# Two weight splits moved ahead of the 16x16 inverses, and each inverse built from two 8x8 ones, in a two-layer hybrid transformer block

## The chip, the cores and the metric

The kernel runs on one core of one Trainium2 chip. The metric is the device time of one execution in microseconds. The core has TensorE (matrix products, "PE" in the profile; its weight loads are "PEld"), VectorE ("DVE"), ScalarE ("ACT"), GpSimd ("POOL") and SyncE ("SP", which only issues transfers). They run side by side and wait for each other by semaphores.

## The reference

Two layers work on 256 latent and 256 context tokens of width 1024. In each layer stand a SwiGLU feed-forward, a mixer of three branches (pooling, a gated delta rule in both directions, attention) whose outputs are weighed by sigmoid gates, and a second feed-forward. The change touches the delta rule and what runs beside it. In the delta rule a unit lower-triangular 64x64 system is solved for each of 4 heads, 8 chunks of 64 tokens and 2 directions:

```
A = jnp.where(tril_strict, beta[..., :, None] * kk * decay_mat, 0.0)
lhs = A + jnp.eye(C, dtype=F32)
rhs = jnp.concatenate([v * beta[..., None], k * (beta * jnp.exp(G))[..., None]], axis=-1)
sol = lax.linalg.triangular_solve(lhs, rhs, left_side=True, lower=True, unit_diagonal=True)
```

Beside it stand the projections of the gates, three of width 1024 out of the columns of `w_in`:

```
ga, gb, gc = jnp.split(jax.nn.sigmoid(gates), N_BRANCH, axis=-1)
m = ga * (y_pool @ wa) + gb * (y_dn @ wb) + gc * (y_att @ wc)
```

## The kernel before

All weights come in blocks of 128x1024 numbers through a ring of four slots. For each block a transfer fills `raw`; ScalarE rounds it into `w_hi` (L802); VectorE makes the remainder `w_lo` (the helper `lower`, L1416); and TensorE multiplies with both halves: the three products of L1978, L1979 and L1980 for each of 8 pieces of a block. One such triple is called a *unit* here; it has 512 columns in layer 0 and 256 in layer 1. A block therefore gives TensorE 8 units, and TensorE waits for its `w_lo` before the first.

The order of the instructions on each engine is written out by hand. The 24 gate blocks of a layer (192 units) are filler: a table (`gate_plan`) says how many units TensorE does at each of a row of "gate points", spread over the mixer. Each engine has its own function `gates(p)`. On TensorE it does the units of point p. On ScalarE it takes the sum of each block that is finished at p out of PSUM (L1028) and rounds the block three further on. On VectorE it makes the lower parts for the blocks that were finished at point p - 1: for gate g finished there, the lower part of block g + 3.

The delta rule runs twice in a layer, for two pairs of heads (w = 0 and 1). So there are four such passes, which the text calls S1 (layer 0, w = 0), S2 (layer 0, w = 1), S3 (layer 1, w = 0) and S4 (layer 1, w = 1). Each has three parts:

- Preparation. ScalarE makes decay matrices (L1149), VectorE the matrices `amT` = A (L1738 to L1748), and TensorE does points 0 to 3 in between. Point 4 follows at once on TensorE, with 13 to 19 units. The text calls them points 0 to 4; the change moves what VectorE does at points 3 and 4.
- The small inverses (`sub_blocks`, L1660 to L1698). The 16x16 blocks on the diagonal of all sixteen 128x128 matrices are packed by VectorE (L1728, partitions 0 to 63) and ScalarE (L1158, partitions 64 to 127), turned so that one partition holds one whole 16x16 block (L1668), and inverted there on VectorE alone by 14 elimination steps of two small instructions each (L1684, L1686). They are turned back (L1690) and spread into `tm` by VectorE (L1696) and ScalarE (L1189).
- The solve. TensorE, which has waited for `low` and `lowa` (the two halves of `tm`), doubles the inverse to 32, 64 in three levels (L2344, L2347, L2355), each with replies of ScalarE (L1198) and VectorE (L1788, L1794). The scan over the chunks follows.

The two semaphore waits that matter for TensorE's place are these, behind its points 3 and 4:

```
gates(delta_point(l, w, 3))
gates(delta_point(l, w, PREP_POINTS))
pe.wait_ge(eax.sem, eax.at(l, 4 * w + 4))
pe.wait_ge(low.sem, low.at(l, w + 1))
pe.wait_ge(lowa.sem, lowa.at(l, w + 1))
```

The table gives these lower parts to VectorE at the two points: at point 3 one in S1 and S4 and none in S2 and S3; at point 4 one in each pass. Before, point 3 stands behind the third of the 14 elimination steps, and point 4 behind the last instruction of `sub_blocks`.

## Time and profile before

| | |
|---|---|
| time, median of 3 runs | 2339.87 us (2334.74 to 2342.08) |
| the profiled execution's own time | 2333.58 us |
| its span in the profile | 2331.9 us |
| TensorE busy | 2208.4 us, 95% of the span |
| VectorE busy | 1374.2 us, 59% |
| ScalarE busy | 882.9 us, 38% |
| mean granted TensorE clock | 0.977 of full speed |
| the four passes, from packed blocks to the start of the solve | near 718, 807, 1924 and 2001 us |

Busy time is time in which an instruction is in execution. An engine's idle time is put down to what released it. TensorE is busy nearly always, so the time of the kernel is the sum of TensorE's work and its waits; waits of the other engines cost nothing unless TensorE waits behind them.

### The profile page before, as it was taken

The numbers are of one execution on the slowest core, as the hardware profiler recorded it, in microseconds if no ns is written. First come the engines' busy times: TensorE is split into PE (matmuls) and PEld (weight loads), VectorE is DVE, ScalarE is ACT, GpSimd is POOL, SyncE is SP. The second block draws the span as 40 slices with busy tenths as digits, with TensorE's granted clock in tenths as the row PEclk, the third lists the DMA queues.
The fourth block names the chain that finished last, engine by engine and source line by source line (L and its number), as shares of the span: only waits on it lengthen the run. The fifth ranks groups of instructions, "written<-read, shape, count | busy, mean of one in ns | idle before, by whom it ended". The sixth has DMA issues, their size and how long they took to land.

```text
span 2331.9 us, 33743 instructions
## 1 busy us (share of the span) xinstructions
PE 2208.4 (95%) x12606; PEld 1851.0 (79%) x12606; DVE 1374.2 (59%) x2353; ACT 882.9 (38%) x1376; POOL 236.3 (10%) x300
## 2 busy tenths in 40 slices
PE   4999999999998989999999999999999997798998
PEld 1888878987567767888888898888889776788998
DVE  5777876634446447478875256555356555665554
ACT  2433322433443325343222243332245552355643
POOL 3000022000000200300001100000110001102001
PEclk8999999999999989999999999999999998899999
DMA  6455554322102205245554334444333311144554
GB/s 258 162 184 195 193 175 130 126 85 93 37 32 68 70 27 199 100 165 196 197 188 128 94 123 148 142 143 138 99 126 119 106 55 48 58 161 149 184 172 145
DMA packets 96448, 303.86 MB, mean 130 GB/s; under 512 B 10592, under 2 KB 17248, under 8 KB 95328
## 3 DMA queue, kind: packets, MB, share of 16 engines
q1 hardware_dynamic: 76912, 230.87, 30.1%
q0 software_dynamic: 18720, 69.21, 8.7%
q10 hardware_dynamic: 720, 2.44, 0.3%
q8 instruction: 67, 1.10, 0.2%
q14 instruction: 29, 0.24, 0.0%
HBM read 291.99 MB, written 10.49 MB: 130 GB/s over the span
## 4 chain that ended last, share of the span: by engine, by line
PE 55%; DVE 4%; ACT 2%; issue 1%; DMA 1%; SPq 0%; ACTq 0%; DVEq 0%
PE ps L1978 16%; PE ps L1980 16%; PE ps L1979 16%; DVE w_lo L1416 1%; PE ps L2229 1%; PE ps L2250 1%; PE ps L2344 1%; PE ps L2355 0%; PE ps L2347 0%; PE ps L2416 0%; PE ps L2414 0%; PE ps L2238 0%; PE ps L2166 0%; DVE gate_in L1871 0%; ACT w_hi L802 0%
## 5 line engine op out<-in xcount | busy, mean ns | idle before, releaser
L1978 PE MATMUL ps<-h_hi,w_hi 128*128 128x512 f32 (+1 forms) x2176 | 781.8, 359 | 61.7 <-DVE w_lo L1416 43.3
L1979 PE MATMUL ps<-h_lo,w_hi 128*128 128x512 f32 (+1 forms) x2176 | 763.7, 351 | 0.0
L1980 PE MATMUL ps<-h_hi,w_lo 128*128 128x512 f32 (+1 forms) x2176 | 763.7, 351 | 0.0
L1416 DVE TENSOR_TENSOR w_lo<-raw,w_hi 128x1024 fp32r<-128x1024 f32 (+2 forms) x416 | 475.2, 1146 | 464.3 <-ACT w_hi L802 458.8
L802 ACT ACTIVATE w_hi<-raw 128x1024 fp32r<-128x1024 f32 (+2 forms) x416 | 404.6, 974 | 619.3 <-DMA raw<-in_w_down 316.9
L1978 PEld LDWEIGHTS ps<-h_hi,w_hi 128*128 128x128 f32 x2176 | 420.4, 193 | 153.5 <-DVE w_lo L1416 47.5
L1980 PEld LDWEIGHTS ps<-h_hi,w_lo 128*128 128x128 f32 x2176 | 420.8, 193 | 52.2
L1979 PEld LDWEIGHTS ps<-h_lo,w_hi 128*128 128x128 f32 x2176 | 421.1, 194 | 49.4
L1978 PE MATMUL ps<-a_hi,w_hi 128*128 128x512 f32 (+1 forms) x1050 | 362.4, 345 | 9.5 <-DVE buf_b L1873 3.6
L1980 PE MATMUL ps<-a_hi,w_lo 128*128 128x512 f32 (+1 forms) x1050 | 360.7, 343 | 0.0
L1979 PE MATMUL ps<-a_lo,w_hi 128*128 128x512 f32 (+1 forms) x1050 | 359.2, 342 | 0.0
L1448 DVE CUSTOM_DVE_ANT_0 ps<-ada,c_wide 128x1024 f32<-128x1024 f32 x256 | 319.4, 1248 | 7.5 <-DMA ada<-in_w_ada_t 2.4
L1978 PEld LDWEIGHTS ps<-a_hi,w_hi 128*128 128x128 f32 x1050 | 197.2, 188 | 38.6 <-DVE buf_b L1873 5.8
L1979 PEld LDWEIGHTS ps<-a_lo,w_hi 128*128 128x128 f32 x1050 | 197.3, 188 | 26.7
L1980 PEld LDWEIGHTS ps<-a_hi,w_lo 128*128 128x128 f32 x1050 | 197.7, 188 | 25.8
L696 POOL DMA_DIRECT2D ada<-in_w_ada_t x128 | 67.9, 531 | 775.3 <-DVE ada_sum L1448 768.1
L920 ACT ACTIVATE a_hi<-buf_b 128x512 f32 (+3 forms) x88 | 50.9, 579 | 204.8 <-DVE buf_b L1434 204.8
L658 POOL TENSOR_TENSOR buf_a<-x 128x512 f32<-128x512 f32 (+1 forms) x40 | 51.8, 1296 | 247.2 <-DVE x L1422 246.4
L1439 DVE TENSOR_TENSOR a_lo<-buf_b,a_hi 128x512 f32 (+3 forms) x88 | 54.7, 622 | 26.2 <-ACT a_hi L920 26.1
L1422 DVE SCALAR_TENSOR_TENSOR x<-ps,mod,x 128x256 f32<-128x256 f32 (+1 forms) x68 | 30.4, 480 | 60.6 <-PE ps L1980 60.6
L1434 DVE TENSOR_TENSOR buf_b<-buf_a,ps 128x512 f32<-128x512 f32 (+1 forms) x88 | 54.1, 615 | 8.2 <-PE ps L1980 8.2
L704 POOL MEMSET tm<- 128x2048 f32 x4 | 7.2, 1806 | 470.7 <-DVE g_cum L1701 470.7
(253 smaller groups left out, 1844.8 us busy)
## 6 DMA issues: line engine op xcount, KB each, us to landing
raw<-in_w_up SPq DMA_DIRECT2D x176, 512.0 KB, 3.8
ada<-in_w_ada_t POOLq DMA_DIRECT2D x128, 512.0 KB, 3.9
raw<-in_w_down SPq DMA_DIRECT2D x64, 384.0 KB, 3.1
raw<-in_w_gate SPq DMA_DIRECT2D x48, 512.0 KB, 3.3
raw<-in_w_down SPq DMA_DIRECT2D x64, 320.0 KB, 2.9
raw<-in_w_proj SPq DMA_DIRECT2D x32, 512.0 KB, 3.3
raw<-in_w_merge SPq DMA_DIRECT2D x16, 512.0 KB, 3.8
raw<-in_w_out SPq DMA_DIRECT2D x16, 512.0 KB, 3.2
```

Source lines behind the costliest of these rows:

```text
L658: link(pool.tensor_tensor(buf_a[:, 1, 0:n], xk, xk, ALU.mult))
L696: pool.dma_start(ada[:, j, :], a["w_ada_t"][ADA_FIRST - KD + 2 * r + j]).then_inc(s_ada[j], 16)
L802: return act.activation(w_hi[:, j % RING, 0:cols], raw[:, j, 0:cols], ACT.Copy)
L920: act.activation(a_hi[:, q, 0:n], buf_b[:, j, 0:n], ACT.Copy).then_inc(s_ahi, 1)
L1416: vec.tensor_tensor(w_lo[:, j % RING, 0:cols], raw[:, j, 0:cols], w_hi[:, j % RING, 0:cols].bitcast(F32), ALU.subtract).then_inc(s_lo, 1)
L1422: last = vec.scalar_tensor_tensor(x[:, k, cols], ps[:, bank, cols], mod[:, l, (3 * which + 2) * KD + k, i:i + 1], x[:, k, cols], ALU.mult, ...
L1434: vec.tensor_tensor(buf_b[:, j, 0:n], buf_a[:, j, 0:n], ps[:, 2 * j + 1, 0:n], ALU.mult).then_inc(s_mul, 1)
L1439: vec.tensor_tensor(a_lo[:, q, 0:n], buf_b[:, j, 0:n], a_hi[:, q, 0:n].bitcast(F32), ALU.subtract).then_inc(s_alo, 1)
L1448: vec.tensor_tensor_reduce(ps[:, 6:8, :].rearrange("p b n -> p (b n)"), ada[:, j, :], c_wide[:, i, :], 1.0, 0.0, ALU.mult, ALU.add, ada_su ...
L1978: pe.matmul(out, wh, rows_hi[:, i, c], start=first, stop=False)
L1979: pe.matmul(out, wh, rows_lo[:, i, c], start=False, stop=False)
L1980: return pe.matmul(out, wl, rows_hi[:, i, c], start=False, stop=last)
```

## The change

It has three parts, all inside `sub_blocks` and the packing ahead of it.

1. Both calls `gates(...)` on VectorE, points 3 and 4, now stand directly behind the set-up of the small inverses and ahead of all elimination steps.
2. The masks with which the turned blocks were taken apart (four instructions over 256 elements) are applied while packing: the copies become multiplications by a column of 0 or -1 (`minus_rows`), on VectorE and on ScalarE. Behind the transposition one addition of two halves takes the place of two masked instructions; the rest of the set-up stays.
3. Each 16x16 inverse is made from two 8x8 ones. Six elimination steps (in place of 14) work on both 8x8 diagonal blocks at once; then the corner is the product of the two inverses with the block between them: two multiplications over 512 elements, each followed by a sum over groups of eight.

```diff
@@ packed
-            to = sub_pack[r, :].rearrange("p (i z t h) -> p z t h i", z=2, t=8, h=2)[:, :, 4 * h:4 * h + 4]
-            old = amT[r, 4 * h:4 * h + 4, r].rearrange("p t (h i) -> p t h i", h=2)
-            return [(to[:, z], old) for z in range(2)]
+            out = []
+            for e in range(2):
+                c = q * QUAD + e * SUB
+                to = sub_pack[r, :].rearrange("p (i z t e) -> p e z t i", z=2, t=8, e=2)[:, e, :, 4 * h:4 * h + 4, :]
+                old = amT[r, 4 * h:4 * h + 4, c:c + SUB].rearrange("p (o t) n -> p o t n", o=1)
+                out.append((to, old.to_broadcast([QUAD, 2, 4, SUB]), minus_rows(e, r)))
+            return out
+        def sub_halves(r0, rows, c0, cols, row_step=SUB, col_step=1):
+            return bass.AP(xm, 2 * P + r0 * SUB + c0, [[8 * P, P], [(SUB + 1) * SUB // 2, 2], [row_step, rows], [col_step, cols]])
+        def sub_terms(at, left):
+            if left:
+                return bass.AP(xm, at, [[8 * P, P], [SUB, SUB // 2], [0, SUB // 2], [1, SUB // 2]])
+            return bass.AP(xm, at, [[8 * P, P], [0, SUB // 2], [1, SUB // 2], [SUB, SUB // 2]])
@@ ScalarE, pack
-                            last = act.activation(to, old, ACT.Copy)
+                            last = act.activation(to, old, ACT.Copy, scale=minus)
@@ VectorE, sub_blocks
-                    link(vec.tensor_scalar(t, raws[:, :, 0, :], half_minus(0, 1), None, ALU.mult))
-                    link(vec.scalar_tensor_tensor(t, raws[:, :, 1, :], half_minus(1, 1), t, ALU.mult, ALU.add))
-                    link(vec.scalar_tensor_tensor(t, raws_t[:, :, 0, :], half_minus(0, 0), t, ALU.mult, ALU.add))
-                    link(vec.scalar_tensor_tensor(t, raws_t[:, :, 1, :], half_minus(1, 0), t, ALU.mult, ALU.add))
+                    link(vec.tensor_tensor(sums, raws[:, :, 0, :], raws[:, :, 1, :], ALU.add))
+                    link(vec.tensor_scalar(sub_t, sub_sum, side_rows(1), None, ALU.mult))
+                    link(vec.scalar_tensor_tensor(t, sub_sum.rearrange("p (i j) -> p j i", i=SUB), side_rows(0), t,
+                                                  ALU.mult, ALU.add))
                     link(vec.tensor_tensor(sub_t, sub_t, low_mask, ALU.mult))
                     link(vec.tensor_copy(sub_t[:, 0:SUB * SUB:SUB + 1], ones[:, 0:SUB]))
-                    for j in range(1, SUB - 1):
-                        if j == SUB // 4:
-                            gates(delta_point(l, w, PREP_POINTS - 1))
-                        size = [P, SUB - 1 - j, j]
-                        part = sub_part[:, 0:size[1] * j].rearrange("p (i c) -> p i c", c=j)
-                        link(vec.tensor_tensor(part, t[:, j + 1:SUB, j:j + 1].to_broadcast(size),
-                                               t[:, j:j + 1, 0:j].to_broadcast(size), ALU.mult))
-                        link(vec.tensor_tensor(t[:, j + 1:SUB, 0:j], t[:, j + 1:SUB, 0:j], part, ALU.add))
+                    gates(delta_point(l, w, PREP_POINTS - 1))
+                    gates(delta_point(l, w, PREP_POINTS))
+                    half = SUB // 2
+                    for j in range(1, half - 1):
+                        rows = half - 1 - j
+                        part = sub_part[:, 0:2 * rows * j].rearrange("p (b i c) -> p b i c", b=2, c=j)
+                        link(vec.tensor_tensor(part, sub_halves(j + 1, rows, j, j, col_step=0),
+                                               sub_halves(j, rows, 0, j, row_step=0), ALU.mult))
+                        link(vec.tensor_tensor(sub_halves(j + 1, rows, 0, j), sub_halves(j + 1, rows, 0, j), part, ALU.add))
+                    corner, last = 2 * P + half * SUB, 2 * P + half * SUB + half
+                    terms = sub_part.rearrange("p (i x k) -> p i x k", i=half, x=half)
+                    made = sub_sum[:, 0:half * SUB].rearrange("p (i x) -> p i x", x=SUB)[:, :, 0:half]
+                    link(vec.tensor_tensor(terms, sub_terms(corner, True), sub_terms(2 * P, False), ALU.mult))
+                    link(vec.tensor_reduce(made, terms, AXX, ALU.add))
+                    link(vec.tensor_tensor(terms, sub_terms(last, True), sub_terms(0, False), ALU.mult))
+                    link(vec.tensor_reduce(t[:, half:SUB, 0:half], terms, AXX, ALU.add))
...
                     last.then_inc(low.sem, 1)
-                    gates(delta_point(l, w, PREP_POINTS))
@@ VectorE, pack
-                            last = vec.tensor_copy(to, old)
+                            last = vec.tensor_scalar(to, old, minus, None, ALU.mult)
```

VectorE in S1, from the set-up of the inverses to the first lower part. `xm` is the memory in which `sub_pack`, `sub_raw`, `sub_sum`, `sub_t` and `sub_part` lie, and `w_lo` rows are the lower parts. Before:

```order
L1674 SCALAR_TENSOR_TENSOR xm<-xm,masks 128x256
L1675 SCALAR_TENSOR_TENSOR xm<-xm,masks 128x256
L1676 SCALAR_TENSOR_TENSOR xm<-xm,masks 128x256
L1677 TENSOR_TENSOR xm<-xm,masks 128x256
L1678 COPY xm<-ones 128x16
L1684 TENSOR_TENSOR xm<-xm 128x14
L1686 TENSOR_TENSOR xm<-xm 128x14
L1684 TENSOR_TENSOR xm<-xm 128x26
L1686 TENSOR_TENSOR xm<-xm 128x13x2
L1684 TENSOR_TENSOR xm<-xm 128x36
L1686 TENSOR_TENSOR xm<-xm 128x12x3
L1416 TENSOR_TENSOR w_lo<-raw,w_hi 128x1024
```

The same place of the change:

```order
L1682 STREAM_TRANSPOSE xm<-xm 128x512
L1686 TENSOR_TENSOR xm<-xm 128x256
L1687 TENSOR_SCALAR xm<-xm,masks 128x256
L1688 SCALAR_TENSOR_TENSOR xm<-xm,masks 128x256
L1690 TENSOR_TENSOR xm<-xm,masks 128x256
L1691 COPY xm<-ones 128x16
L1430 TENSOR_TENSOR w_lo<-raw,w_hi 128x1024 x2
L1698 TENSOR_TENSOR xm<-xm 128x12
L1700 TENSOR_TENSOR xm<-xm 128x2x6
```

The set-up has one instruction less, and two lower parts in a row stand where the first elimination step stood.

VectorE in S1, the end of `sub_blocks` up to the first reply to the solve. Before:

```order
L1684 TENSOR_TENSOR xm<-xm 128x14
L1686 TENSOR_TENSOR xm<-xm 128x14
L1687 TENSOR_SCALAR xm<-xm,masks 128x256
L1688 SCALAR_TENSOR_TENSOR xm<-xm,masks 128x256
L1690 STREAM_TRANSPOSE xm<-xm 128x512
L1692 ISA
L1696 TENSOR_SCALAR tm<-xm,masks 32x16x16 x5
L1416 TENSOR_TENSOR w_lo<-raw,w_hi 128x1024
L1788 TENSOR_TENSOR xm<-ps,masks 128x512 x2
```

And of the change:

```order
L1698 TENSOR_TENSOR xm<-xm 128x12
L1700 TENSOR_TENSOR xm<-xm 128x2x6
L1704 TENSOR_TENSOR xm<-xm 128x512
L1705 TENSOR_REDUCE xm<-xm 128x8x8
L1706 TENSOR_TENSOR xm<-xm 128x512
L1707 TENSOR_REDUCE xm<-xm 128x8x8
L1708 TENSOR_SCALAR xm<-xm,masks 128x256
L1709 SCALAR_TENSOR_TENSOR xm<-xm,masks 128x256
L1711 STREAM_TRANSPOSE xm<-xm 128x512
L1713 ISA
L1717 TENSOR_SCALAR tm<-xm,masks 32x16x16 x5
L1808 TENSOR_TENSOR xm<-ps,masks 128x512 x2
```

The four instructions of the corner are new, the tail is the same, and no lower part stands behind it any more. TensorE's, ScalarE's and GpSimd's rows stand in the order of before; ScalarE's packing reads `masks` as well.

## Rows read from the trace of the kernel before

**Rows 1.** The page, the chain that ended last, shares by engine.

```profile
PE 55%; DVE 4%; ACT 2%; issue 1%; DMA 1%; SPq 0%; ACTq 0%; DVEq 0%
```

**Rows 2.** PE's waits in 690:850 and 1850:2100: us in total, times, longest.

```profile
PE ps L1978 <- DVE w_lo L1416: 14.3, 3, 8.2
...
PE ps L1978 <- DVE w_lo L1416: 23.6, 3, 12.3
```

**Rows 3.** Timeline of PE in S1: start us, us, engine, line, names, shape, count.

```profile
720.83 0.39 PE L1980 MATMUL ps<-h_hi,w_lo 128*128 128x512 f32 x1
...
721.51 0.39 PE L1980 MATMUL ps<-h_hi,w_lo 128*128 128x512 f32 x1
724.73 0.50 PE L1978 MATMUL ps<-h_hi,w_hi 128*128 128x512 f32 x1 [2.83 <-DVE w_lo L1416]
...
735.33 0.50 PE L1978 MATMUL ps<-h_hi,w_hi 128*128 128x512 f32 x1 [3.27 <-DVE w_lo L1416]
...
740.46 1.03 PE L2344 MATMUL ps<-consts,tm 128*128 128x128 f32 x8
...
745.93 1.04 PE L2344 MATMUL ps<-consts,tm 128*128 128x128 f32 x8
```

**Rows 4.** Timeline of DVE in S1.

```profile
718.31 0.70 DVE L1668 STREAM_TRANSPOSE xm<-xm 128x512 f32<-128x512 f32 x1
...
722.11 0.17 DVE L1684 TENSOR_TENSOR xm<-xm 128x14 f32<-128x14 f32 x1
...
723.45 1.23 DVE L1416 TENSOR_TENSOR w_lo<-raw,w_hi 128x1024 fp32r<-128x1024 f32 x1
724.59 0.20 DVE L1684 TENSOR_TENSOR xm<-xm 128x44 f32<-128x44 f32 x1
...
729.86 0.35 DVE L1687 TENSOR_SCALAR xm<-xm,masks 128x256 f32<-128x256 f32 x1
```

**Rows 5.** Timeline of ACT in S1.

```profile
715.42 2.79 ACT L1158 ACTIVATE xm<-amT 32x128 f32<-32x128 f32 x8
...
732.14 2.06 ACT L1189 ACTIVATE tm<-xm,masks 32x256 f32<-32x256 f32 x3 [8.67 <-DVEq L1692]
```

**Rows 6.** Timeline of PE in S2, S3 and S4.

```profile
823.13 0.80 PE L1978 MATMUL ps<-h_hi,w_hi 128*128 128x512 f32 x1 [8.17 <-DVE w_lo L1416]
...
830.34 1.03 PE L2344 MATMUL ps<-consts,tm 128*128 128x128 f32 x8
...
1940.22 0.58 PE L1978 MATMUL ps<-h_hi,w_hi 128*128 128x256 f32 x1 [12.29 <-DVE w_lo L1416]
...
1943.59 1.36 PE L2344 MATMUL ps<-consts,tm 128*128 128x128 f32 x8
...
2007.05 0.58 PE L1978 MATMUL ps<-h_hi,w_hi 128*128 128x256 f32 x1 [6.20 <-DVE w_lo L1416]
...
2017.62 0.58 PE L1978 MATMUL ps<-h_hi,w_hi 128*128 128x256 f32 x1 [5.09 <-DVE w_lo L1416]
2018.43 1.91 PE L2344 MATMUL ps<-consts,tm 128*128 128x128 f32 x8
...
2026.00 1.04 PE L2344 MATMUL ps<-consts,tm 128*128 128x128 f32 x8
```

**Rows 7.** Groups by line and shape: count, busy us, mean ns, idle before.

```profile
L1633 DVE TENSOR_REDUCE stat<-ps 128x1 f32<-128x512 f32 x32 | 22.1, 690 | 20.2 <-PE ps L2229 20.1
L1738 DVE TENSOR_TENSOR amT<-em,beta 128x512 f32<-128x512 f32 x8 | 5.5, 691 | 27.2 <-ACT em L1149 27.2
L1675 DVE SCALAR_TENSOR_TENSOR xm<-xm,masks 128x256 f32<-128x256 f32 x4 | 2.8, 688 | 0.1
L1674 DVE SCALAR_TENSOR_TENSOR xm<-xm,masks 128x256 f32<-128x256 f32 x4 | 1.9, 485 | 0.1
...
L832 ACT ACTIVATE out_t<-buf_a,nfin 128x256 f32<-128x256 f32 x8 | 3.6, 500 | 1.7 <-DVE buf_a L1316 1.5
L859 ACT ACTIVATE buf_b<-x 128x256 f32<-128x256 f32 x8 | 3.3, 417 | 31.3 <-DVE x L1335 31.3
```

More of the change, by code:

```diff
@@ L192, in side_rows, with minus_rows @@
             return masks[:, C_HALF - N_KEEP + 2 + z:C_HALF - N_KEEP + 3 + z]
-        def half_minus(h, z):
-            return masks[:, C_HALF - N_KEEP + 4 + 2 * h + z:C_HALF - N_KEEP + 5 + 2 * h + z]
+        def minus_rows(h, r):
+            return masks[r, C_HALF - N_KEEP + 4 + h:C_HALF - N_KEEP + 5 + h]
         def half_rows(h, r):
@@ L1156, in pack @@
                     for q in range(PACKED, len(quads)):
-                        for to, old in packed(h, q):
-                            last = act.activation(to, old, ACT.Copy)
+                        for to, old, minus in packed(h, q):
+                            last = act.activation(to, old, ACT.Copy, scale=minus)
                     last.then_inc(cmp.sem, 1)
@@ L1669, in sub_blocks @@
                     raws = sub_raw.rearrange("p (i h j) -> p i h j", i=SUB, h=2)
-                    raws_t = sub_raw.rearrange("p (i h j) -> p j h i", i=SUB, h=2)
                     sums = sub_sum.rearrange("p (i j) -> p i j", i=SUB)
                     t = sub_t.rearrange("p (i j) -> p i j", i=SUB)
-                    link(vec.tensor_scalar(t, raws[:, :, 0, :], half_minus(0, 1), None, ALU.mult))
-                    link(vec.scalar_tensor_tensor(t, raws[:, :, 1, :], half_minus(1, 1), t, ALU.mult, ALU.add))
@@ L1726, in pack @@
                     for q in range(PACKED):
-                        for to, old in packed(h, q):
-                            last = vec.tensor_copy(to, old)
+                        for to, old, minus in packed(h, q):
+                            last = vec.tensor_scalar(to, old, minus, None, ALU.mult)
                     link(last)
@@ L2512, in constants @@
         c[:, C_HALF + 2 + h] = i // SUB % 2 == h
-        for z in range(2):
-            c[:, C_HALF + 4 + 2 * h + z] = -1.0 * ((i % 2 == h) & (i // SUB % 2 == z))
+        c[:, C_HALF + 4 + h] = -1.0 * (i // SUB % 2 == h)
     s = np.arange(SUB)
```

## The prediction

> **What bounds the kernel now.** I read the chain that ended last first: TensorE holds most of it [rows 1]. So a change pays where TensorE waits, and only there. The table of who waited for whom, taken over both mixers, names one large cause: six waits for a lower part `w_lo`, 14.3 + 23.6 = 37.9 us [rows 2]. The timelines then show where they lie: all six stand inside or right behind the small inverses of the four passes S1 to S4 [rows 3, 6].
>
> S1 shows the pattern. TensorE runs units at 0.68 us each (720.83 to 721.51), stops at 721.90 for the lower part of point 3, restarts at 724.73 when VectorE's L1416 of 723.45 ends, does 8 units, stops again at 732.06 for the lower part of point 4 and restarts at 735.33 [rows 3, 4]. It does the last 5 units and begins the solve at 740.46 without any wait. The inverses themselves are ready before that: ScalarE's half of `tm` ends at 732.14 + 2.06 = 734.20 [rows 5]. So now the gate block is late and the inverse is not. If the block comes earlier, the inverse is late next. That exchange is what has to be worked out.
>
> A second cost sits on top of each wait. The 8 units behind 724.73 take 7.33 us, where 8 x 0.68 = 5.44 would do, and the 5 units behind 735.33 take 5.13 for 3.40 [rows 3]. So a restart after some 3 us of idleness costs TensorE a further 1.7 to 1.9 us, and one after 8.17 us costs 7.21 - 7 x 0.68 = 2.4 us [rows 6]. The solve suffers too: in S4, 0.8 us behind a restart, its first level takes 2026.00 - 2018.43 = 7.57 us, and in S1, with TensorE undisturbed, 745.93 - 740.46 = 5.47 us [rows 3, 6].
>
> **The change, part by part.** I count from T, the start of VectorE's transposition (718.31 in S1).
>
> *Packing.* The same number of instructions over the same elements, now with a scale. On VectorE I set this at nothing. On ScalarE a copy of 256 elements with a scale column takes 0.500 us and a plain activation 0.417 [rows 7], so +0.083 us each. In S1 eight copies run into T back to back (2.79 us from 715.42, ending 0.1 us before T) [rows 5]: T comes 0.6 us later. Elsewhere four copies count: 0.3 us. The other bound is nothing at all, since the scaled copies of L1189, twice as long, take 2.06 / 3 = 0.69 us, no more than two of L1158 at 0.35 [rows 5].
>
> *Set-up.* It took 722.11 - 718.31 = 3.80 us [rows 4]. One of the two instructions that read across rows goes (0.688) [rows 7]; the others keep their size or shrink slightly: 3.1 us.
>
> *Lower parts.* An L1416 occupies VectorE 724.59 - 723.45 = 1.14 us, and TensorE restarts 1.28 us after its start [rows 3, 4]. S1 and S4 now have two in front of the inverses, S2 and S3 one. Their inputs: ScalarE's order is unchanged, and in S1 its packing ends at 718.2, so the two roundings that stand next in its order come before VectorE gets to their lower parts, at 722.0 and 723.1.
>
> *Elimination.* 28 small instructions took 729.86 - 722.11 - 1.14 = 6.61 us, 0.236 each [rows 4]. Twelve remain, with fewer elements but one more dimension: 12 x 0.236 = 2.8 us.
>
> *Corner.* The trace has no such product. The nearest from below is an ordinary 512-element product, 0.691 us. But its right operand steps by 16 numbers per element. L1675, which reads that way, takes 0.688 for 256 elements, L1674 beside it 0.485: 0.203 us more per 256 [rows 7]. So 0.691 + 2 x 0.203 = 1.10 us, which I take because the pattern is the same; from above, twice L1675, 1.38. A sum over 512 elements takes 0.690 (L1633, to one result) [rows 7]; with 64 results I take the same, and 1.10 from above. Together 2 x 1.10 + 2 x 0.69 = 3.6, with the links between them 3.7 us; between 2.8 and 5.0.
>
> The Trainium skill ("VectorE: DVE Perf Modes", the section on the TRN2 errata) gives (N + 151) / 0.96 ns for such a product whatever its pattern, so 0.69 us. For 256 elements it would give 0.42, and L1675 shows 0.688, so the rows speak against it here. By it the corner would be 0.8 us shorter in each pass and the gain 3.3 us larger. "SBUF — State Buffer", the section "Door 1: The DMA port swizzle", says that reads that leave a 16-byte line at every element pay a penalty, which is the rows' side.
>
> *Tail.* Unchanged: 734.20 - 729.86 = 4.34 us up to ScalarE's half [rows 4, 5], and 0.1 us to TensorE.
>
> Sum from T to the solve's release: 3.1 + 2.8 + 3.7 + 4.3 + 0.1 = 14.0, plus 1.14 for each lower part in front: 16.3 us in S1 and S4, 15.2 in S2 and S3, plus the 0.6 or 0.3 of packing. Before, TensorE's last restart stood 735.33 - 718.31 = 17.02 us behind T in S1. S4 has the same instructions; S2 and S3 have one L1416 less, 15.88. That gives the old T of the other passes from their restarts [rows 6].
>
> - S1: solve at 718.31 + 16.3 + 0.6 = 735.2, before 740.46: 5.3 us earlier. TensorE's units would be done at 732.1 (restart at 718.31 + 0.6 + 3.1 + 1.28 = 723.3, then 13 x 0.68), so it waits 3.1 us for the inverse.
> - S2: 823.13 - 15.88 + 15.5 = 822.8, before 830.34: 7.6 us. TensorE's block is there in time (it was wanted at 823.13 - 8.17 = 814.96, the lower part ends near 812), 7 units end at 819.7, and it waits 3.0 us.
> - S3: 1940.22 - 15.88 + 15.5 = 1939.8, before 1943.59: 3.8 us. TensorE waits some 8 us.
> - S4: 2017.62 - 17.02 + 16.6 = 2017.2, before 2018.43: 1.2 us. The first wait of 6.20 shrinks to about 4.4 (restart at 2000.6 + 0.3 + 3.1 + 1.28), and another of 6 us stands before the solve.
>
> Together 17.9 us. In all four passes the solve now waits for the inverse, so it begins behind an idle TensorE, and the slow restart falls into it: 1.7 us in S1 and in S2 (waits of 3 us). In S3 2.1 us, what S4 shows over S1: a level right behind a restart would lose a little more, and S3's lost a little already (1.36 for 1.03 in its first row), which I take as equal. In S4 0.4 more than now. Together 5.9 us. The dips that the units no longer have are in the starts above already.
>
> Net 17.9 - 5.9 = 12.0 us. Moved transfers: the order of their issue is unchanged and slots become free earlier, so I cost them at nothing; TensorE's wait would show if they were late. Behind the solve all is as before and TensorE is the bound, so the 12.0 us should stay. Profiled execution: 2333.58 - 12.0 = 2321.6 us. It ran 6.3 us below the median, so for a median 2339.87 - 12.0 = **2328 us**.
>
> **Rivals.**
> - *Forecast* (0.70): the inverse becomes the late one in each pass; 8 to 16 us, 2324 to 2332.
> - *The short chain* (0.14): products at the 0.69 us of L1738 (-3.3 us over four passes), steps at 0.21 (-1.2), no price for the scale (-1.5), and 3 us of idleness not slowing a solve whose products stand between replies anyway (-3.4): 21 us, 2318.5. For it: the solve's products are short. Against it: L1675.
> - *Only the gate wait pays* (0.12): products at 1.38, sums at 1.10 (+5.5 us over the passes), and a slow restart after the remaining 1.4 us wait in S1 (+1.9): a gain of 4.6, 2335. Within 0.3% (7 us, about what a measurement can tell).
> - *The corner eats it* (0.04): the corner's four instructions lie behind both lower parts and in front of `low`, and every us there delays all four solves. At 3.0 us above my 3.7 the gain is gone; at 4.8 above, 8.5 in all, the kernel is 7 us slower: 2347. That needs products of some 3.5 us each, five times an ordinary one; nothing in the rows reads that badly.
> - That the gate blocks don't come earlier at all would need ScalarE's rounding over 1 us late; the order forbids it.
>
> The likeliest is 2328; the range 2317 to 2335 takes in the short chain and most of the third case. Faster by over 0.3%: 0.84; within: 0.12; slower: 0.04.
>
> **What would show it.** In the profile after, the waits for `w_lo` in both mixers should fall from 37.9 to about 7 us (1.4 in S1, 1.1 in S3, 4.4 in S4, none in S2), and four waits of TensorE for `tm` should appear in front of the solve, of 3, 3, 8 and 6 us. The transposition should come 0.3 to 0.6 us later behind ScalarE, the products should take 1.1 us, the sums 0.7, and the first level of the solve 7 us or more in place of 5.5. The prediction is wrong if a product takes over 2 us, if the restart costs nothing, or if the freed time turns up as a wait behind the mixer.

## The result and the profile after

| | before | changed kernel |
|---|---|---|
| median of the first comparison, us | 2337.88 (2334.74 to 2342.08, 4 runs) | 2316.32 (2311.71 to 2319.58, 4 runs) |
| ratio | | 0.9913, 95% interval 0.9893 to 0.9933 |
| profiled execution: span / time, us | 2331.9 / 2333.58 | 2315.7 / 2317.6 |
| mean granted clock | 0.977 | 0.981 |

The change makes the kernel faster by 0.9%. Forecast were 2328 us and a range from 2317; it came out 11.7 us below the first and just under the second. With all later comparisons the kernel before has a median of 2333.9 (76 runs) and the changed one 2317.0 (16 runs in three sets): the gain is 17 us, with a 95% interval of 15.7 to 19.0 from resampling the two sets. The first four runs of before were high ones, so the 21.6 us between the first two medians say too much.

The table of waits, PE alone, in the stretches 690:870 and 1850:2100 of the changed kernel, answers [rows 2]:

```profile
PE ps L2364 <- ACT tm L1203: 5.1, 2, 2.6
PE ps L2422 <- DVE vnew L1833: 1.8, 2, 1.5
PE ps L1998 <- DVE w_lo L1430: 1.1, 1, 1.1
...
PE ps L2364 <- ACT tm L1203: 14.9, 2, 8.3
PE ps L1998 <- DVE w_lo L1430: 5.1, 2, 4.4
```

The waits for `w_lo` fell from 37.9 to 6.2 us, and four waits of the solve (L2364) for `tm` took their place, 20.0 us in all: block and inverse have exchanged roles. The wait for `vnew` is not new; in the kernel before it stands at 860.02 us with 1.53 us, just outside the stretch read there. VectorE's timeline in S1 (start us, us, line, names, shape, count) answers [rows 4]:

```profile
717.53 0.71 DVE L1682 STREAM_TRANSPOSE xm<-xm 128x512 f32<-128x512 f32 x1
...
720.51 2.36 DVE L1430 TENSOR_TENSOR w_lo<-raw,w_hi 128x1024 fp32r<-128x1024 f32 x2
722.79 0.17 DVE L1698 TENSOR_TENSOR xm<-xm 128x12 f32<-128x12 f32 x1
...
725.34 1.05 DVE L1704 TENSOR_TENSOR xm<-xm 128x512 f32<-128x512 f32 x1
726.43 0.69 DVE L1705 TENSOR_REDUCE xm<-xm 128x64 f32<-128x512 f32 x1
727.15 1.05 DVE L1706 TENSOR_TENSOR xm<-xm 128x512 f32<-128x512 f32 x1
728.24 0.69 DVE L1707 TENSOR_REDUCE xm<-xm 128x64 f32<-128x512 f32 x1
728.96 0.35 DVE L1708 TENSOR_SCALAR xm<-xm,masks 128x256 f32<-128x256 f32 x1
```

From T at 717.53: set-up 2.98 us, two lower parts 2.28, twelve steps 2.55, corner 3.62. ScalarE in the same place answers [rows 5]:

```profile
714.21 3.30 ACT L1172 ACTIVATE xm<-amT,masks 32x128 f32<-32x128 f32 x8
...
731.24 2.06 ACT L1203 ACTIVATE tm<-xm,masks 32x256 f32<-32x256 f32 x3 [8.97 <-DVEq L1713]
```

Eight scaled copies take 3.30 us where eight plain ones took 2.79. TensorE in S1, S2 and S4 answers [rows 3, 6]; the wait ahead of an instruction stands in brackets:

```profile
721.79 0.50 PE L1998 MATMUL ps<-h_hi,w_hi 128*128 128x512 f32 x1 [1.10 <-DVE w_lo L1430]
...
733.44 1.06 PE L2364 MATMUL ps<-consts,tm 128*128 128x128 f32 x8 [2.48 <-ACT tm L1203]
...
740.59 1.04 PE L2364 MATMUL ps<-consts,tm 128*128 128x128 f32 x8
...
816.97 1.94 PE L2364 MATMUL ps<-consts,tm 128*128 128x128 f32 x8 [2.58 <-ACT tm L1203]
...
1987.29 0.48 PE L1998 MATMUL ps<-h_hi,w_hi 128*128 128x256 f32 x1 [4.41 <-DVE w_lo L1430]
...
1998.87 1.94 PE L2364 MATMUL ps<-consts,tm 128*128 128x128 f32 x8 [6.59 <-ACT tm L1203]
```

The same eight first products of the solve take 1.03 us undisturbed [rows 3] and 1.94 behind the waits of S2 and S4. Windows over the first level of the solve in S1 to S4 (length, then busy us of each engine with counts, then granted clock, DMA share, GB/s) show why:

```profile
733.44:740.59 7.15, 7.15 (x48) 7.07 (x49) 2.07 (x3) 2.73 (x4) 0.00 (x0) 0.76 0.10 37
816.97:823.95 6.98, 6.98 (x48) 6.90 (x49) 2.07 (x3) 2.73 (x4) 0.00 (x0) 0.78 0.10 38
1922.76:1929.81 7.05, 7.05 (x49) 6.97 (x49) 2.07 (x3) 2.51 (x4) 0.00 (x0) 0.77 0.07 21
1998.87:2007.08 8.21, 8.21 (x48) 8.13 (x49) 2.07 (x3) 2.52 (x4) 0.00 (x0) 0.66 0.06 18
```

and of the kernel before, where S1 and S4 stand for the two cases:

```profile
740.46:745.93 5.47, 5.47 (x49) 5.39 (x48) 2.07 (x3) 2.25 (x3) 0.00 (x0) 1.00 0.00 0
...
2018.43:2026.00 7.57, 7.57 (x50) 7.49 (x49) 2.07 (x3) 2.25 (x3) 0.00 (x0) 0.71 0.01 2
```

The "slow restart" of the prediction is the clock: a level that runs wholly at the full level (2.4 GHz, 1.00) takes 5.47 us, and one that spends about half of its time or more at the lower (1.2 GHz) takes 7 or more.

To compare kernels whose passes stand at other places, I measure each pass by itself, from the first product of its third group of decay rows (703.09 us in S1 of the kernel before; TensorE does gate point 0 ahead of it) to the start of the solve and to the second level. From the timelines of the two kernels, in us:

```
                 to the solve: S1    S2    S3    S4     to its second level: S1    S2    S3    S4    sum
before                      37.37 38.28 29.77 29.04                       42.84 43.75 35.57 36.61  158.8
changed                     31.56 30.22 25.53 27.44                       38.72 37.21 32.58 35.65  144.2
```

The solve starts 5.8, 8.1, 4.2 and 1.6 us earlier in its pass (19.7 together), its first level gives back 5.1, and 14.6 remain. TensorE's last product comes 16.2 us earlier (2322.9 and 2306.7). The stretch up to that product in S1 (703.1 and 701.9) was 1.2 us of this, the rest between and behind the passes 0.4, both of unchanged work.

### The profile page after: what moved, and what is told of

Read it like the earlier page. It is cut to its first block, busy times and chain, and to the rows that moved or that the text cites. A ratio compares the mean times of both kernels' runs of the same rounds, so it can differ in the third digit from the quotient of the medians.

```text
span 2315.7 us, 33693 instructions
## 1 busy us (share of the span) xinstructions
PE 2204.7 (95%) x12606; PEld 1848.5 (80%) x12606; DVE 1372.9 (59%) x2301; ACT 884.4 (38%) x1376; POOL 236.1 (10%) x300
## 4 chain that ended last, share of the span: by engine, by line
PE 56%; DVE 4%; ACT 2%; DMA 1%; issue 1%; SPq 0%; ACTq 0%; DVEq 0%
PE ps L1998 17%; PE ps L2000 16%; PE ps L1999 16%; DVE w_lo L1430 1%; PE ps L2249 1%; PE ps L2270 1%; PE ps L2364 1%; PE ps L2367 1%; PE ps L2375 1%; PE ps L2436 0%; PE ps L2434 0%; DMA gate_in<-gate_sums 0%; PE ps L2258 0%; PE ps L2314 0%; PE ps L2186 0%
## 5 line engine op out<-in xcount | busy, mean ns | idle before, releaser
L1998 PE MATMUL ps<-h_hi,w_hi 128*128 128x512 f32 (+1 forms) x2176 | 775.4, 356 | 30.1 <-DVE w_lo L1430 11.7
```

What stands on the lines that cost most here:

```text
L1998: pe.matmul(out, wh, rows_hi[:, i, c], start=first, stop=False)
```

## The experiments

They ran in four sets, each on one chip with its own runs of the kernel before. The table has for each the parts of its profile and its times, in us: the profile up to the start of the first pass, the four passes as above, everything else up to TensorE's last product, and the medians.

```
                                up to S1  passes   else    median (runs)      ratio, 95% interval
kernel before                    703.1    158.8   1461.0
before again                     702.6    160.4   1467.2   2334.36 (12)       1.0002  0.9985-1.0018
change                           701.9    144.2   1460.7   2316.32 (4)        0.9913  0.9893-0.9933
change again                     703.1    144.5   1457.8   2316.30 (6)        0.9923  0.9902-0.9945
change, third                    705.7    143.7   1460.4   2317.62 (6)        0.9931  0.9911-0.9950
lower parts only                 703.3    147.3   1457.0   2321.55 (10)       0.9952  0.9935-0.9969
lower parts only, again          701.4    148.5   1456.6   2317.46 (6)        0.9937  0.9917-0.9958
inverse and packing only         703.4    153.5   1468.6   2336.04 (12)       1.0003  0.9986-1.0019
old packing                      702.1    148.3   1456.3   2318.41 (4)        0.9932  0.9909-0.9956
corner made longer               701.0    157.8   1467.8   2336.11 (10)       1.0005  0.9989-1.0021
corner in another order          704.2    143.5   1461.2   2318.97 (4)        0.9935  0.9912-0.9957
change + fill                    702.6    137.5   1459.9   2311.77 (6)        0.9910  0.9892-0.9929
change + fill, again             705.0    137.6   1460.4   2313.24 (6)        0.9912  0.9895-0.9930
lower parts + fill               701.7    141.2   1460.1   2312.04 (5)        0.9905  0.9889-0.9921
lower parts + fill, again        699.6    141.3   1459.8   2312.55 (6)        0.9914  0.9895-0.9932
change + fill + fill in a scan   704.0    137.6   1459.9   2314.19 (6)        0.9916  0.9900-0.9932
before + fill                    700.6    152.9   1469.8   2329.05 (12)       0.9975  0.9963-0.9987
```

The passes repeat within 1.6 us for one kernel; the other two columns, where all kernels do the same work, vary by 6 and 13. A single profile shows a pass well and the total badly.

### The change again, and before again

No edit. 

> The changed kernel once more, in more rounds. The two profiles at hand give the four delta passes a gain of 14.6 us (each pass from its own packing to the second level of its solve) and the rest of the program 1.6 us, while the medians lie 20 to 22 us apart. Theory A (the passes are all, the rest is the chance of single executions): ratio 0.9935 to 0.9945, so 13 to 15 us, and a second profile whose passes repeat those of the first within 0.5 us each. Theory B (something outside the passes gains 5 us or more in most executions): ratio near 0.9913 again.

> The kernel before itself, for a second profile and for what two equal kernels differ by. Ratio 1.000 within 0.002. Theory A: its passes repeat the first profile's within 0.5 us each, and the rest of the program differs from it by several us, at places where TensorE restarts slowly by chance. Theory B: the rest repeats as well.

The change repeated its gain at ratio 0.9923, between the two theories; its passes came out at 144.5 us in all, with S3's 0.9 us longer, more than the 0.5 expected. The kernel before repeated itself (1.0002). In its second profile the passes differ by 1.6 us, S1's by 1.3 and not the 0.5 expected, and the rest by 6.2. Where the 6.2 comes from is visible in the scan behind S2. Windows over its first 300 products, the same in every kernel, of before and of before again:

```profile
835.85:876.58 40.73, 38.95 (x303) 30.60 (x301) 17.88 (x40) 10.33 (x18) 4.54 (x10) 0.92 0.06 21
```

```profile
836.98:882.82 45.84, 44.05 (x302) 33.05 (x301) 17.88 (x40) 10.33 (x18) 4.55 (x10) 0.79 0.06 18
```

The same work takes 5.1 us more at a mean clock of 0.79 than at 0.92. Windows over the first 600 products of this place, in the change, in before again and in the kernel with the lower parts alone (below):

```profile
823.95:929.50 105.55, 101.86 (x603) 81.16 (x601) 65.46 (x94) 43.65 (x54) 4.54 (x10) 0.97 0.36 123
```

```profile
837.00:949.91 112.91, 109.22 (x602) 85.22 (x601) 65.44 (x94) 43.75 (x54) 4.55 (x10) 0.89 0.34 115
```

```profile
827.28:930.85 103.57, 98.97 (x603) 79.44 (x602) 65.44 (x94) 43.69 (x54) 4.54 (x10) 1.00 0.37 125
```

This is less a matter of chance than it looks. The 600 products took 105.5 us in all three profiles of the change and in all four of the fill with early lower parts, 103.6 in both of the lower parts alone, in the old packing and in the other order of the corner. Only the kernel before, among those profiled more than once, shows two values (105.6 and 112.9). The inverse alone, the long corner and before with fill took 110.0 to 111.4.

### The two halves of the change

The lower parts ahead, with the old packing, set-up and elimination:

```diff
+                    gates(delta_point(l, w, PREP_POINTS - 1))
+                    gates(delta_point(l, w, PREP_POINTS))
                     for j in range(1, SUB - 1):
-                        if j == SUB // 4:
-                            gates(delta_point(l, w, PREP_POINTS - 1))
...
-                    gates(delta_point(l, w, PREP_POINTS))
```

> Part 1 of the change alone: both lower parts stand ahead of the 14 elimination steps, packing and inverse are those of before. From the transposition to the solve: 3.80 set-up + 1.14 for each lower part + 6.61 steps + 4.34 tail + 0.1 = 17.1 us in S1 and S4, 16.0 in S2 and S3. The solve would start 5.0, 7.1, 3.2 and 0.6 us earlier than before, 15.9 us together, less 5 us for slow restarts in the solve: 11 us, three quarters of the passes' 14.6. If instead the shorter inverse were what pays, this would gain under 4 us.

And the new packing and inverse with the lower parts where they were:

```diff
-                    gates(delta_point(l, w, PREP_POINTS - 1))
-                    gates(delta_point(l, w, PREP_POINTS))
                     for j in range(1, half - 1):
+                        if j == SUB // 4:
+                            gates(delta_point(l, w, PREP_POINTS - 1))
...
+                    gates(delta_point(l, w, PREP_POINTS))
```

> Parts 2 and 3 alone: masks in the packing and 8x8 inverses, with the lower parts where they stood before (behind the third elimination step, and behind the end). The last restart of TensorE comes 0.4 (packing) + 3.0 + 1.1 (where there is a part at point 3) + 2.55 + 3.62 + 4.2 + 1.3 behind the old transposition: 16.2 us in S1 and S4 and 15.1 in S2 and S3, where it was 17.02 and 15.88. So about 0.8 us in each pass, 3.2 us in all, within 0.3% or barely over. If the inverse's length is what counts, it would gain over 8 us.

The lower parts alone bring 2321.55 and, in a second set, 2317.46: 2320.3 over 16 runs, 14 of the 17 us. The starts of the solve moved by 5.0, 7.1, 3.2 and 0.7 us, as expected. Its waits in the two stretches are those of the change with a longer wait for `tm`:

```profile
PE ps L2343 <- ACT tm L1189: 6.5, 2, 3.6
...
PE ps L2343 <- ACT tm L1189: 15.1, 2, 8.8
PE ps L1977 <- DVE w_lo L1416: 6.4, 2, 4.9
```

The inverse alone brings nothing (1.0003): the waits for `w_lo` are still 12.4 + 22.4 us, since the last block stands behind an inverse that is only a little shorter. Its passes are 5.3 us shorter in the profile (3.2 were expected), and the rest of that execution is 7.6 us longer, with 45.1 us for the 300 products behind S2. So whether the shorter passes are a gain that chance covers can't be read from one profile; twelve timed runs show none.

### The packing's share

The change with the plain copies and the four masked instructions of before, and the new inverse:

```diff
-                            last = act.activation(to, old, ACT.Copy, scale=minus)
+                            last = act.activation(to, old, ACT.Copy)
-                    link(vec.tensor_tensor(sums, raws[:, :, 0, :], raws[:, :, 1, :], ALU.add))
-                    link(vec.tensor_scalar(sub_t, sub_sum, side_rows(1), None, ALU.mult))
...
+                    link(vec.tensor_scalar(t, raws[:, :, 0, :], half_minus(0, 1), None, ALU.mult))
+                    link(vec.scalar_tensor_tensor(t, raws[:, :, 1, :], half_minus(1, 1), t, ALU.mult, ALU.add))
...
```

> The change without its part 2: copies in the packing and four masked instructions behind the transposition, as before; the 8x8 halves and both lower parts ahead of them stay. ScalarE's packing ends 0.3 to 0.5 us earlier, the set-up takes 3.8 in place of 3.0 us: the solve starts 0.4 us later in each pass, 1.6 us in all, ratio 0.993. If the scaled copies cost what they save, or more, this equals or beats the changed kernel.

The solve starts 0.41, 0.56, 0.50 and 0.49 us later, 2.0 us together: the new packing wins this, the shorter set-up less its own price. The time (0.9932 beside 0.9913, 0.9923 and 0.9931 for the change) can't tell 2 us.

### The corner, made longer and turned round

The last rival named the corner as the one place that could turn the gain into a loss. Two products and a sum done twice make it 2.9 us longer:

```diff
                     link(vec.tensor_reduce(made, terms, AXX, ALU.add))
                     link(vec.tensor_tensor(terms, sub_terms(last, True), sub_terms(0, False), ALU.mult))
+                    link(vec.tensor_tensor(terms, sub_terms(corner, True), sub_terms(2 * P, False), ALU.mult))
+                    link(vec.tensor_reduce(made, terms, AXX, ALU.add))
+                    link(vec.tensor_tensor(terms, sub_terms(last, True), sub_terms(0, False), ALU.mult))
```

> The changed kernel with three of the corner's instructions done twice, with the same operands and results: a product, its sum and the other product, 1.05 + 0.69 + 1.05 + 0.1 for the links = 2.9 us more in each pass. Theory: the inverse is the last thing before the solve in all four passes, so all of it is on the path: 11.6 us more than the changed kernel, ratio near 0.9975. If TensorE's own units still ended last in some pass, that pass would take nothing from it, and the loss would be 8.7 us or less.

The solves start 2.9, 2.9, 2.9 and 2.8 us later, microsecond for microsecond, and the first levels lose another 2. The passes take 13.6 us more, and the time is back at that of before (1.0005). That is 19 us more than the change and not the 11.6 expected: the rest of the profile is 7.1 us longer too, 4.4 of it in the 600 products behind S2. The corner stands on the path in all four passes. The rival's turning point, 3.0 us above the forecast, came true as a number; the corner's own 11.4 us would have left some 6 us of the gain, and the clock took the rest.

The other edit turns the order of the products round, so that it is the sum that reads in steps and not the product:

```diff
-                return bass.AP(xm, at, [[8 * P, P], [SUB, SUB // 2], [0, SUB // 2], [1, SUB // 2]])
+                return bass.AP(xm, at, [[8 * P, P], [SUB, SUB // 2], [1, SUB // 2], [0, SUB // 2]])
...
-                    terms = sub_part.rearrange("p (i x k) -> p i x k", i=half, x=half)
+                    terms = sub_part.rearrange("p (i k x) -> p i k x", i=half, x=half)
+                    terms_x = sub_part.rearrange("p (i k x) -> p i x k", i=half, x=half)
```

> The changed kernel, with the corner's terms laid out so that both products read and write runs of eight neighbours, and the sums step by eight numbers in their place. If it is the read that steps at every element that costs a product 1.05 in place of 0.69 us: products 0.69, and the sums rise from 0.69 to about 1.05, with the total unchanged at 3.6 us. If the sum doesn't mind, the corner takes 2.9 us, 0.7 less per pass and 2.9 us in all.

Groups by line and shape, first of the change, then of this kernel:

```profile
L1704 DVE TENSOR_TENSOR xm<-xm 128x512 f32<-128x512 f32 x4 | 4.2, 1042 | 0.1
L1706 DVE TENSOR_TENSOR xm<-xm 128x512 f32<-128x512 f32 x4 | 4.1, 1034 | 0.1
L1705 DVE TENSOR_REDUCE xm<-xm 128x64 f32<-128x512 f32 x4 | 2.7, 686 | 0.1
```

```profile
L1706 DVE TENSOR_REDUCE xm<-xm 128x64 f32<-128x512 f32 x4 | 4.4, 1105 | 0.1
...
L1705 DVE TENSOR_TENSOR xm<-xm 128x512 f32<-128x512 f32 x4 | 2.8, 692 | 0.1
```

The product falls from 1.04 to 0.69 us and the sum rises from 0.69 to 1.10: the price of the stepped read moves with the read, and the corner stays at 3.6 us.

This kernel shows one thing more. TensorE at the start of the solve in S2, and the window over its first level:

```profile
819.56 1.06 PE L2365 MATMUL ps<-consts,tm 128*128 128x128 f32 x8 [2.73 <-ACT tm L1203]
```

```profile
819.56:825.06 5.50, 5.50 (x48) 5.42 (x49) 2.07 (x3) 2.73 (x4) 0.00 (x0) 1.00 0.13 48
```

Behind a wait of 2.73 us, longer than the 2.58 us of the change in S2, this level ran wholly at the full clock. It is the only one: the other 31 first levels of the eight profiles without fill in which the solve waits for the inverse took 6.9 to 8.4 us. So such a wait nearly always brings the low clock here, and not always.

### Filling TensorE's waits

If the slow first levels come from the idleness ahead of them, TensorE only has to be kept busy. These kernels put products whose result nobody reads into bank 2, free at that point, in front of the waits:

```diff
+                def fill(n):
+                    for _ in range(n):
+                        pe.matmul(ps[:, 2, :], ident_r, h_hi[:, 0, :], start=True, stop=True)
...
+                    fill((10, 11, 35, 35)[2 * l + w])
                     pe.wait_ge(low.sem, low.at(l, w + 1))
```

and 18 more in front of one block of S4.

> The changed kernel, and while TensorE waits for the inverse it multiplies the identity with a tile of the layer's input into a bank that the solve then overwrites (10, 11, 35 and 35 products of 512 columns in S1 to S4), and 18 more in S4 while it waits for the lower part. The products' results are not used. If idleness of TensorE is what brings the slow restarts: the solve's first level falls from 7.0 to 8.2 us to about 5.5 in all four passes, S4's units behind the lower part run at 0.36 each, the low clock near the passes is gone from the profile, and the kernel gains some 7 to 9 us over the changed one (ratio to before near 0.989). If the clock falls for another reason: no gain, or a loss where the added products delay the solve.

TensorE in S1, with the ten products and what is left of the wait:

```profile
731.54 2.49 PE L2185 MATMUL ps<-h_hi,masks_r 128*128 128x512 f32 x10
734.31 0.41 PE L2373 MATMUL ps<-consts,tm 128*128 128x128 f32 x2 [0.28 <-ACT tm L1203]
```

and the windows over the first levels:

```profile
734.31:739.81 5.50, 5.50 (x48) 5.42 (x49) 2.07 (x3) 2.73 (x4) 0.00 (x0) 1.00 0.13 48
...
1995.93:2001.43 5.50, 5.50 (x48) 5.42 (x49) 2.07 (x3) 2.52 (x4) 0.00 (x0) 1.00 0.09 27
```

5.50 us and clock 1.00 in all four passes, with the solves starting within 0.3 us of where they did. The passes become 6.6 us shorter, and over two sets the time is 2312.7 (12 runs) against 2317.0: 4.2 us, interval 2.3 to 5.8, less than the 7 to 9 expected. So the price of the restarts was the clock's, and it can be had back.

The same for the kernel before, which waits elsewhere:

```diff
+                fills = {(0, 14): 11, (0, 15): 13, (0, 21): 34, (1, 14): 52, (1, 20): 25, (1, 21): 29}
...
+                            if (l, g) in fills:
+                                pe.wait_ge(eax.sem, eax.at(l, 4 if g < 20 and (l, g) != (0, 21) else 8))
+                                fill(fills[l, g])
                             pe.wait_ge(s_lo, b + 1)
```

> The kernel before, with 11, 13, 34, 52, 25 and 29 products of 512 columns that nobody reads, put where TensorE waits longest for w_lo of the third and fourth gate point; nothing else is changed. Theory (the low clock of the solves comes from the idleness ahead of them, and its price of 1.7, 2.1, 1.8 and 2.5 us in the four first levels can be had back without any gain on VectorE): first levels 5.5 us in each pass where they read 5.5 to 7.6, the time at the low clock down from 92.7 us by 20 or more, solve starts unmoved within 0.3 us, gate blocks ahead of the solve faster too; about 2325, ratio 0.9965. Rival (in the kernel before the blocks between the waits bring the clock back in time, so filling gives nothing, and each product that runs on past the arrival of w_lo costs): 2333 to 2336, ratio 1.000 to 1.001.

All first levels take 5.47 us and S2's solve starts 2.1 us earlier, S3's 1.3. S1 gave nothing (42.96 for 42.84). The expectation set a price of 1.7 and 2.1 us on the first levels of S1 and S2, which already took 5.47; what S2 gave lies ahead of its solve. Over the whole execution the time at the low clock fell from 108 us (the expectation had 92.7) to 90. The passes are 5.9 us shorter, the ratio is 0.9975 (0.9963 to 0.9987), 5.8 us. Filling alone is worth a third of what the change gives, and it does not replace it: with the fill in both, the kernel before has 2329.05 and the changed one 2312.7, still 16 us apart.

Six more fill products in S2's scan, where TensorE waits 1.5 us for `vnew`, on top of the fill of the change:

```diff
                             gates(delta_point(l, w, PREP_POINTS + 2 * t))
+                            if l == 0 and w == 1 and t == 1:
+                                fill(6)
                             pe.wait_ge(vn.sem, vn.at(l, 3 * w + t))
```

> The change with the fill of before, and 6 more such products in the second pass's scan, where TensorE waits 1.5 us for the new values of the second tile and a stretch of 7 to 24 us at the low clock follows in each profile so far. Theory (that short idleness starts the long low stretches behind the second pass): granted clock 1.00 from there to the end of the scan, 3 to 4 us less in the profile, 2309 against 2311.8, ratio 0.9895. Rival (the low stretch has another start, and the 6 products add at most their own end): the low stretch is still there, 2311.8 to 2312.5.

Windows over the 300 products behind S2, of the change with fill and of this kernel:

```profile
821.77:862.47 40.70, 38.91 (x302) 30.50 (x302) 17.87 (x40) 10.33 (x18) 4.55 (x10) 0.92 0.07 20
```

```profile
823.17:861.94 38.77, 37.49 (x308) 29.96 (x308) 17.88 (x40) 10.34 (x18) 4.55 (x10) 1.00 0.07 21
...
861.94:905.00 43.06, 41.16 (x202) 33.01 (x203) 28.20 (x35) 22.65 (x25) 0.00 (x0) 0.96 0.57 196
```

The low stretch is gone from there (1.9 us), but the clock fell later in the same scan (0.96), and the time is not better: 2314.19. The lower parts alone (38.76 us at 1.00, twice), the old packing and the corner in another order have the same wait of 1.5 us there and no low clock behind it, so the wait by itself does not bring it. In the other kernels without these six products the clock falls within 3 us behind the wait. Whether it takes part is neither shown nor excluded; as a means of gaining time the fill here failed.

### What the new inverse is worth

With the fill the price of the clock is out of the way, so the two halves can be compared again. The edit is the fill (14, 14, 38, 38 and 20 products) in the kernel with the lower parts alone.

> Lower parts early with the inverse and packing of before, and such products (14, 14, 38, 38 ahead of the solve, 20 in front of one block of the last pass). Beside the same fill with the whole change (2311.8) it shows what the new inverse is worth where the clock is no matter. Theory: what it is worth is the start of the solve, 0.8 to 1.0 us in each pass, 3.7 in all: 2315.5, ratio 0.9925; first levels 5.5 us. Rival (the 5.2 us between the lower parts alone and the whole change was mostly the shorter idle stretch ahead of the solve, which the fill gives anyway): 2312, ratio 0.991.

> The whole change with the fill, again. Both theories: 2311.8, ratio 0.991.

> The lower parts alone with the fill, again. Theory P (the inverse pays what it starts the solve earlier, 3.7 us, whatever the clock does): 3.7 us above the whole change with the fill, ratio 0.9925. Rival C (it pays mostly by the shorter idle stretch ahead of the solve): within 1.5 us of the whole change with the fill, ratio 0.991.

> The change, a third time. Both theories: 4.5 us above the fill, 2316.3, ratio 0.992.

> The lower parts alone, again. Theory P: 3.7 us and the difference of the restarts (first levels 5.5 to 7.4 in both), so 4 above the change, 2320, ratio 0.994. Rival C: 5 to 6 above it, 2321.5 to 2322, ratio 0.995.

In the profile the theory holds each time: the solves start 0.8, 1.0, 1.0 and 0.9 us later with the old inverse, first levels are at 1.00, the passes 3.7 us longer. In the times it fails: 2312.0 for the lower parts (11 runs) and 2312.7 for the change (12 runs), a difference of -0.7 us with an interval of -1.9 to 1.7, where 3.7 were expected. Without the fill the two sets disagree (5.2 us and -0.2); pooled it is 3.4, interval 0.9 to 6.8. The rival, that the inverse pays by the shorter idle stretch, would explain the filled times and the first set without fill, but not the second set (-0.2) and not the profiles, where the first levels without the fill are nearly alike in both kernels (29.4 us in the change, 28.8 and 30.0 with the lower parts alone).

The unchanged stretch up to S1 took 702.6, 705.0 and 704.0 us in the three filled profiles with the new inverse and 701.7 and 699.6 in the two with the old. Windows over 430:442 in it, change with fill and lower parts with fill:

```profile
430.00:442.00 12.00, 10.57 (x65) 10.37 (x64) 4.80 (x9) 5.64 (x12) 0.00 (x0) 0.72 0.64 225
```

```profile
430.00:442.00 12.00, 9.71 (x80) 9.42 (x80) 7.31 (x15) 7.01 (x16) 0.00 (x0) 1.00 0.72 254
```

The low stretch there costs about 3 us and cancels the inverse's gain in these profiles. It also came in one of two profiles of the kernel before and of the lower parts alone, and in two of three of the change. Whether it is chance or depends on the kernel stays open. So the new inverse is shown to be worth 3.7 us in the passes, and no gain of it is shown in the times.

## Why the prediction was right and where it was wrong

**Right: the exchange.** Waits for `w_lo` 6.2 us (forecast 7), four waits for `tm` of 2.5, 2.6, 8.3 and 6.6 us (3, 3, 8 and 6), the order of causes, and no new wait behind the mixer. Lower parts only and inverse only confirm it apart: most of the gain is the block's.

**Right: the corner.** Products 1.04 us (1.10), sums 0.69 (0.69), in all 3.62 (3.7). Turning the order shows that the stepped read is the price. The row it was priced by, L1675, reads with a step of 32 numbers and not of 16; the size came out near all the same. (N + 151) / 0.96 from the Trainium skill ("VectorE: DVE Perf Modes", the section on the TRN2 errata) gives 0.69 us for a product over 512 elements and has no term for a step; it holds for the unstepped product (692 ns) and misses the stepped one by 0.35 us. Corner made longer shows that this term had full weight.

**Mis-sized by little: from T to the solve.** The forecast had 16.3 us in S1; it took 15.9: set-up 2.98 (3.1), steps 2.55 (2.8), corner 3.62 (3.7). T came 0.43 us later in its pass, not 0.6. The starts moved by 5.8, 8.1, 4.2 and 1.6 us in place of 5.3, 7.6, 3.8 and 1.2: 19.7 for 17.9.

**Mis-sized by little: the slow restart.** Forecast 5.9, measured 5.1 (1.7, 1.5, 1.3, 0.6). The wait of 2.5 us was enough for the full price, against the short chain's assumption, though one wait of 2.73 us in the other order of the corner cost nothing. In all 24 first levels of the six filled profiles the clock was 1.00, so TensorE's idleness is what brings the low clock here, and the clock is all of the price.

**The step that failed: "for a median 2339.87 - 12.0".** The mechanism held, but both terms of this sum were mis-sized, and together the forecast was 11.7 us too high: 6 from the anchor, 2.6 from the passes and about 3 from a term set at nothing.

- The anchor, 2339.87. The three runs shown had their median 6 us above that of the 76 runs of all comparisons (2333.9). The profiled execution's own 2333.58 was the better estimate: with the same 12.0 it would have given 2321.6, 5 us above the result in place of 12.
- The 12.0, "Net 17.9 - 5.9 = 12.0 us". Both of its terms erred to the same side, so the passes gave 19.7 - 5.1 = 14.6 us (15.9 between the repetitions of both kernels).
- "Behind the solve all is as before", a term set at nothing. The remainder to the 17 us of the pooled times, 1 to 2.5 us, lies outside the passes (3 us to the median of the first comparison). The work there is as before, the clock is not. The stretch took 1456.3 to 1461.2 us in the twelve profiles whose lower parts come early and whose corner is not lengthened, and 1461.0 to 1469.8 in the other five: the kernel before twice, once with fill, the inverse alone, the long corner. Most of this lies in one place, the 600 products behind S2: 103.6 to 105.5 us in the twelve, and 105.6, 112.9, 111.4, 111.4 and 110.0 in the five. Fewer low stretches there fit the remainder; what sets them was not isolated.

**The rivals.** The short chain named a time near the measured one, 2318.5 us, and that was luck: neither the products nor the restart were free, and of its terms only the steps of 0.21 us came true. Only the gate wait pays, and the corner eats it, did not come about. With 2.9 us more in the corner the gain was gone, as the turning point of the latter said, though only 11.4 of the 19 us were the corner's own delay.

## What to carry to other kernels

When two things are late in turn, put the cheaper one first and then price the other as the new wait, with everything on its engine between it and the wait; here that gave each start within 0.6 us. Where TensorE waits ahead of a chain of short products, as here for 2.5 us and more, look at the granted clock of the chain in the windows: if it is below 1.00, products that nobody reads, in a bank that is free, gave back what it cost (4 us here, and 6 in the kernel before). Judge a change of a few us by the stretch it touches and by many timed runs together, and anchor a forecast at more than three of them.

## What the runs showed that I had not expected

- The same 300 products behind S2 took 38.8, 40.7, 43.6, 45.1 or 45.8 us, by the granted clock alone (1.00, 0.92, ..., 0.79), in kernels that are alike there, and nearly the same in each profile of one kernel, save the kernel before. Up to the first pass, too, the same work took from 699.6 to 705.7 us.
- A sum over 512 elements with a stepped read takes 1.10 us and a product 1.04, against 0.69 for both without: the price of the step is that of the read, 0.34 to 0.42 us, whichever instruction has it.
- A copy of 32 x 128 with a scale column costs VectorE 329 ns against 270 for the plain copy, and ScalarE 3.30 against 2.79 us for eight.
- Behind waits of about the same length the clock was low from the first product on in S2 (eight in 1.94 us) and only behind the first eight in S1 (1.06 us); the price of the whole level was nearly the same. Behind one such wait, of 2.73 us, it was not low at all.
